# Second RMSNorm of a streaming encoder layer: adding up the squared feature tiles on GpSimd, and one sum over the partitions on TensorE

## The reference, cut to what matters

```python
def rmsnorm(x, g):
    xf = x.astype(jnp.float32)
    y = xf * lax.rsqrt(jnp.mean(xf * xf, axis=-1, keepdims=True) + RMS_EPS)
    return (y * g.astype(jnp.float32)).astype(x.dtype)
...
    x = x + gt1 * (merged @ w_out)
    h2 = rmsnorm(x, g_norm[1]) * (1 + sc2) + sh2
    u, gg = jnp.split(h2 @ w_ffn_in, 2, axis=-1)
    x = x + gt2 * ((jax.nn.silu(gg) * u) @ w_ffn_out)
```

## Time and profile before

| | |
|---|---|
| median of 3 runs | 1036.46 us (1035.94 to 1036.84) |
| span of the profiled execution | 1034.1 us |
| TensorE busy | 995.1 us, 96% |
| VectorE busy | 521.6 us, 50% |
| ScalarE busy | 447.0 us, 43% |
| GpSimd busy | 359.7 us, 35% |
| mean granted TensorE clock | 0.997 |

### The profile page before, as it was taken

How to read it: one execution, slowest core, us unless ns; L and a number is a source line. 1 busy time by engine, 2 the same in 40 slices (tenths; PEclk the granted TensorE clock), 3 DMA queues, 4 the chain that set the end, 5 groups by cost and what they waited for, 6 DMA issues and landing times.

```text
span 1034.1 us, 26814 instructions
## 1 busy us (share of the span) xinstructions
PE 995.1 (96%) x10988; PEld 914.6 (88%) x10988; DVE 521.6 (50%) x1200; ACT 447.0 (43%) x991; POOL 359.7 (35%) x318
## 2 busy tenths in 40 slices
PE   6999999999999989998899999999999999999996
PEld 4899999899998666776788999999999999999996
DVE  4500000078006666666547756888888887800003
ACT  4433323354345444554432355555555556711113
POOL 1164344342332433600252354333233342133330
PEclk9999999999999999999999999999999999999998
DMA  9986756334412000002332632232423323232212
GB/s 356 395 299 228 247 189 212 107 126 148 137 45 60 13 14 13 14 24 76 126 98 85 204 122 82 74 90 82 121 81 95 108 81 97 60 110 85 84 57 87
DMA packets 118182, 122.33 MB, mean 118 GB/s; under 512 B 5396, under 2 KB 102848, under 8 KB 115656
## 3 DMA queue, kind: packets, MB, share of 16 engines
q1 hardware_dynamic: 112864, 111.86, 33.2%
q10 hardware_dynamic: 5224, 9.10, 2.7%
HBM read 108.33 MB, written 15.23 MB: 119 GB/s over the span
## 4 chain that ended last, share of the span: by engine, by line
PE 85%; DVE 7%; ACT 4%; issue 2%; POOL 1%; ACTq 1%; DVEq 0%; POOLq 0%
PE ps L1964 60%; PE ps L2586 21%; PE ps L2328 1%; DVE s_sb L1542 1%; PE ps L2228 1%; DVE hl L1356 1%; DVE Pb L1513 1%; ACT x_sq L871 0%; POOL w_lo L685 0%; DVE XX L1523 0%; PE ps L2619 0%; POOL w_lo L839 0%; ACTq L857 0%; DVE rbx L1369 0%; PE ps L2115 0%
## 5 line engine op out<-in xcount | busy, mean ns | idle before, releaser
L1964 PE MATMUL ps<-hh,w_hi 128*128 128x274 f32 x832 | 176.1, 294 | 1.5 <-DVE hl L1356 0.7
L685 POOL TENSOR_TENSOR w_lo<-w_raw,w_hi 128x2048 fp32r<-128x2048 f32 x22 | 101.4, 4607 | 213.9 <-ACT w_hi L881 197.2
L1964 PE MATMUL ps<-hl,w_hi 128*128 128x274 f32 x832 | 172.9, 290 | 1.0 <-DVE al L1878 1.0
L1964 PE MATMUL ps<-hh,w_lo 128*128 128x274 f32 x832 | 173.2, 290 | 0.0
L1964 PEld LDWEIGHTS ps<-hh,w_hi 128*128 128x128 f32 x832 | 131.5, 189 | 11.7 <-issue 9.9
L1964 PEld LDWEIGHTS ps<-hl,w_hi 128*128 128x128 f32 x832 | 131.5, 189 | 1.2 <-DVE al L1878 1.2
L1964 PEld LDWEIGHTS ps<-hh,w_lo 128*128 128x128 f32 x832 | 131.6, 190 | 0.8 <-issue 0.8
L833 POOL TENSOR_TENSOR ws_lo<-w_raw,ws_hi 128x512 fp32r<-128x512 f32 x63 | 80.6, 1294 | 144.8 <-DVE ps L1796 130.3
L2586 PE MATMUL ps<-th,ws_hi 128*128 128x274 f32 x336 | 97.5, 290 | 0.0
L2586 PE MATMUL ps<-tl,ws_hi 128*128 128x274 f32 x336 | 97.4, 290 | 0.0
L2586 PE MATMUL ps<-th,ws_lo 128*128 128x274 f32 x336 | 97.1, 289 | 0.0
(11 more groups left out here) (438 smaller groups left out, 2288.0 us busy)
## 6 DMA issues: line engine op xcount, KB each, us to landing
w_raw<-in_w_ffn_in SPq DMA_DIRECT2D x44, 512.0 KB, 4.5
w_raw<-in_w_in SPq DMA_DIRECT2D x42, 512.0 KB, 5.0
ada_l<-in_w_ada SPq DMA_DIRECT2D x16, 1024.0 KB, 6.6
ada_w<-in_w_ada SPq DMA_DIRECT2D x8, 1024.0 KB, 13.4
w_raw<-in_w_ffn_out SPq DMA_DIRECT2D x16, 384.0 KB, 3.9
w_raw<-in_w_ffn_out SPq DMA_DIRECT2D x16, 320.0 KB, 3.2
g_d<-gst SPq DMA_DIRECT2D x16, 274.0 KB, 2.2
gring<-g_d SPq DMA_DIRECT2D x16, 274.0 KB, 3.2
```

Of the source, the lines that this page charges most:

```text
L685: pool.tensor_tensor(w_lo[:, s, 0:cols], w_raw[:, s, 0:cols], w_hi[:, s, 0:cols].bitcast(F32), ALU.subtract).then_inc(lo_done, 1)
L1964: return pe.matmul(out, lhsT, rhs, start=start, stop=stop)
```

## The change

ScalarE squares tile 0 straight into a new buffer `sq_sum`, and GpSimd adds the squares of tiles 1 to 7 to it (`add_squares`), all in SBUF. The adds stand ahead of `token_low(c)`, those of tiles 2c and 2c+1. Each one after the first waits for the one before. TensorE sums `sq_sum` over the partitions once, ahead of the fourth k step of the first up unit, into banks 4 and 7. ScalarE's squares from k = 3 on wait for add k-2, which frees the buffer, and no longer for TensorE. On VectorE `raw_sums` of the first unit of seven products goes ahead of the mean, and the mean is two operations, one per bank. The semaphore `rows_in` is used again for the adds.

```diff
+        sq_sum = at("sq_sum", [P, W], E + 13312)
...
+        sq_added, SQ_ADDED = rows_in, 16 * 11
...
+            def add_squares(k):
+
+                pool.wait_ge(sq_done, KS + k + 1)
+                if k > 1:
+                    pool.wait_ge(sq_added, SQ_ADDED + k - 1)
+                pool.tensor_tensor(sq_sum[:, :], sq_sum[:, :], sq_a[:, k % 2, :], ALU.add).then_inc(sq_added, 1)
+
             def token_low(c):
 
+                for k in range(max(1, 2 * c), 2 * c + 2):
+                    add_squares(k)
                 pool.wait_ge(th_done, TH + c + 1)
...
-                if k >= 2:
-                    act.wait_ge(ss_mm, k - 1)
-                act.activation(sq_a[:, k % 2, :], xT[:, k, :], ACT.Square).then_inc(sq_done, 1)
+                if k >= 3:
+                    act.wait_ge(sq_added, SQ_ADDED + k - 2)
+                act.activation(sq_a[:, k % 2, :] if k else sq_sum[:, :], xT[:, k, :], ACT.Square).then_inc(sq_done, 1)
...
-            dve.wait_ge(ss_mm, KD)
-            link(sts(halves(rstd2[:, :]), pair(2), 1.0 / D, RMS_EPS, ALU.mult, ALU.add))
-            dve.reciprocal(rstd2[:, :], rstd2[:, :]).then_inc(var_ready, 1)
...
             raw_sums(U_ST, U_ST % 2)
+            dve.wait_ge(ss_mm, 1)
+            for h in range(2):
+                i = sts(rstd2[:, h * H:(h + 1) * H], ps[:, 4 + 3 * h, 0:H], 1.0 / D, RMS_EPS, ALU.mult, ALU.add)
+            link(i)
+            dve.reciprocal(rstd2[:, :], rstd2[:, :]).then_inc(var_ready, 1)
             second_sums(U_ST, U_ST % 2)
...
-            def sum_square(k):
-
-                pe.wait_ge(sq_done, KS + k + 1)
+            def sum_squares():
+
+                pe.wait_ge(sq_added, SQ_ADDED + KD - 1)
                 for h in range(2):
-                    ins = mm(ps[:, 4 + h, 0:H], ones[:, :], sq_a[:, k % 2, h * H:(h + 1) * H], k == 0, k == KD - 1)
+                    ins = mm(ps[:, 4 + 3 * h, 0:H], ones[:, :], sq_sum[:, h * H:(h + 1) * H])
                 ins.then_inc(ss_mm, 1)
...
-                if i:
-                    sum_square(2 * i - 2)
-                    sum_square(2 * i - 1)
-            sum_square(KD - 2)
             pe.wait_ge(lo_done, U_UP + 1)
             pe.wait_ge(pair_free, T_UP - 1)
             for k in range(KD):
-                if k == 2:
-                    sum_square(KD - 1)
+                if k == 3:
+                    sum_squares()
```

## The result

| | before | changed |
|---|---|---|
| median of 4 runs | 1036.65 us | 1043.76 us (1042.61 to 1044.96) |
| ratio, 95% interval | | 1.0064 (1.0051 to 1.0077) |
| span of the profiled execution | 1034.1 us | 1041.4 us |
| first product matmul (line 2586, now 2595) | 656.01 | 663.09 |
| from there to the end of the span | 378.1 us | 378.3 us |

A forecast was written before the change was run, and what follows sets the result against it. TensorE was taken as the bound, VectorE as the stage's second. Turns and tail 5.3 us plus clock 0.6 made 5.9; 1036.46 + 5.9 = 1042.4 us, range 1038.4 to 1044.6.

The forecast's parts named there:

- What bounds the kernel: Weight-unit stage, 598 to 666 us: VectorE is second bound, 12.3 us per pair of tiles against TensorE's 12.25 a unit.
- The turns: VectorE token sums behind low_in_four: each GpSimd add met costs 1.1 us; residual(2), (4), (7) late by 1.1, 3.2, 5.3.
- What TensorE does then: Unit U_WO+2 starts at 613.6, U_WO+3 at 628.0, the up unit 4.5 us later, after a wait until 647.0.
- The tail: End of the norm: add 7 costs 1.1, raw_sums end at 653.3, mean at 653.4, products at 661.3, 5.3 us later.
- Weight sums ahead of the mean: Norm's tail on VectorE: moving raw_sums is worth 1.2 us behind the mean and costs 1.2 ahead of it.
- nothing, or under 1 us: Sign at the norm's mean on VectorE: it waits for nothing on TensorE, or under 1 us.
- The clock: First up unit: TensorE's clock at half for 3.0 us after idling, 1.5 us of matmul lost, mean 0.6 later.
- rival 4: First up unit: clock at half for all 6.7 us idled, 3.35 lost, 1044.3 us; within the forecast's own range, no separate chance.

The follow-up runs named there:

- e1: Changed kernel without its seven adds, so seven of eight squares are left out of the mean; 1037.38 us beside 1037.44 for the kernel before.
- e6: Kernel before, with first and third token sums in one instruction and the last three low_in_four in eight pieces; ratio 1.0009.
- e7: Changed kernel with e4's held-back adds and e6's shorter VectorE work; 1035.30 us beside 1036.70 for the kernel before, ratio 0.9986.
- e9: e8 without its 16 transposes; 1034.43 us beside 1033.88 for e8, ratio 0.9968 to the kernel before.
- e8: e7 with adds 6 and 7 right behind 4 and 5, last two token_low behind raw_sums, 16 transposes in TensorE's wait; 1033.88 us, ratio 0.9962.
- e2: Kernel before plus only the seven GpSimd adds, into a buffer nobody reads, TensorE keeping all its squares; 1042.10 us, ratio 1.0046.
- e5: Changed kernel with unused transposes (14, 14 and 48) in TensorE's waits for residuals; 1042.15 us beside 1045.02 for the changed kernel.
- e3: Kernel before with only raw_sums moved ahead of the mean and the column sums in banks 4 and 7; ratio 0.9990.
- e4: Changed kernel with the adds of tiles 1 to 5 held back until the last token sum of their pair; 1039.12 us, ratio 1.0016.
- the changed kernel again: The changed kernel, unaltered, measured once more beside e5, e6 and e7 on one chip; 1045.02 us, ratio 1.0076 to the kernel before.

## Why the prediction was right, step by step

- **What bounds the kernel.** Right. With VectorE untouched, TensorE's 6.4 us less gave nothing (e1); with TensorE untouched, VectorE's 1.1 us less per pair gave nothing (e6); both together gave 1.9 us (e7), 2.3 with the last meetings out (e9), and 3.4 with the clock kept up too (e8). The two arrive together, and neither alone is "the" bound.
- **The turns.** The 1.1 us per meeting held: residual(2), (4) and (7) came 1.2, 3.4 and 5.2 us later, for 1.1, 3.2 and 5.3, and e2 gives 5.1 us for the adds alone. That the 5.2 is so near its 5.3 is partly luck: the five token sums were 5.6 us longer together (1.17, 1.18, 1.05, 1.18 and 1.03), and `hl` of tile 5, which took 1.57 us before and 1.24 after, and the wait ahead of it gave 0.4 back. The traces agree with the rule of the Trainium skill that I had named ("SBUF — State Buffer", section "Who interferes with whom"): a token sum with two SBUF inputs waited for the whole of GpSimd's instruction, 1.60 us for 0.43. Residual(7), with one input in PSUM, ran from 645.56 to 646.84 beside an add that GpSimd had from 645.00 to 646.84, and its three operations took the 0.49, 0.47 and 0.25 us that they took before.
- **What TensorE does then.** U_WO+2 at 613.75 (613.6), U_WO+3 at 628.23 (628.0), the up unit at 646.95 (647.0).
- **The tail.** The first of the last token sums met add 7 (1.60 us), raw_sums ended at 653.28 (653.3). Had the column sums been there, the mean would have started where the forecast had it. In e5 it did, at 653.17.
- **Weight sums ahead of the mean.** Forecast as worth nothing in the changed kernel, since the mean would wait for VectorE. It waited for TensorE instead, 1.97 us behind the end of raw_sums, where the prediction had named "nothing, or under 1 us" as its sign. So the two sums lay in a wait, and moving them should have saved about their 1.2 us: an estimate, which no run tests. e3 shows 0.0 for the move in the kernel before.
- **The clock: the term that was too small.** I had taken 3.0 us at half, as long as the fall had taken at the end of the kernel, and 1.5 us lost. It was at half from 645.8 to 652.6, 5.6 us of it with TensorE at work, and 2.5 us were lost: 7.2 us from the first up matmul to the column sums, 4.7 in e5. The sums ended at 655.2 instead of 654.0, and the mean began 1.25 us after the forecast. e5 prices the clock at 1.9 us, where I had 0.6; the turns cost 5.0 there, where I had 5.3. So the clock's term was 1.3 too small, the other 0.3 too large, and 5.9 us were forecast for the 7.1 measured. What came is rival 4's condition (at half for 6.7 us; 6.8 measured) at less than its price (3.35 us lost), since 1.2 us of it passed before TensorE started and a matmul at half clock took 1.8 times as long and not twice. Nothing in the trace of before could give the length, and the range had room for it because rival 4 had been worked out.
- What I would not have got from this sum: the other drop of the clock, in U_WO+2. It cost nothing, since residual(4) came later than the slowed unit.

## What to carry to other kernels

Before work is moved from a busy engine to an idle one, ask what the busy engine's work lies over: 6.4 us of TensorE's matmuls covered waits for VectorE, and taking them off gave nothing. GpSimd with operands in SBUF is not free even when it is idle: each add that met a VectorE instruction with two SBUF inputs held it off for nearly the add's own length, here 1.0 to 1.2 us, so place such work beside VectorE's PSUM work, or cut it short. And when two engines arrive together, shorten both; look at TensorE's idle gaps too: behind those of 2.1 us and more its matmuls ran at half clock here.

## What the runs showed of the hardware

**The clock falls behind shorter waits than I had thought, and with a delay.** In the changed kernel TensorE idled 2.09 us ahead of 613.75, ran 1.3 us of matmuls at full clock, and was put to half at 615.0, until 618.5. In e7, e2 and e9 the clock fell behind waits of 2.31, 2.35 and 2.42 us, in e1 behind 3.99. A wait of 0.92 us (e1) or 0.99 (e5) left it at 1.00. The stretch at half lasted 3.4 us in e1, e2, e7, e9 and at 615, and 6.8 us behind the waits of 6.22 us (changed kernel) and 4.90 us (e4). Whether the length of the wait or its moment decides between the two, these runs don't tell. Nor is the wait ahead of a fall the whole of it: at about 470 us, in a stage that is the same in all these kernels and has no wait of TensorE over 0.5 us just before, the clock fell in three of the twelve profiles (e8, e9 and the changed kernel again) and stayed at 1.00 in the other nine. Some fp32 transposes of 0.11 to 0.12 us each in the wait, results unused, kept the clock up in e5 and e8.

**The turns go both ways.** In the kernel before low_in_four's first pieces start 1.25 us apart (604.31, 605.57, 606.81), which makes 5.0 us for four, but with VectorE's turns in them the four take 5.74; in eight pieces low_in_four takes 7.00 (e7), while VectorE's share gets shorter. The smaller piece moves the cost from VectorE to GpSimd.
